# A product-key expert layer on one core: 40 tokens in row dots, two chunks searched together, and the x rows stored in five pieces

## What is computed

```python
q = (xf @ w_query).reshape(t, PEER_HEADS, 2, HALF_QUERY)            # 512 tokens, 8 heads, two halves
scores = jnp.einsum('thpk,hpnk->thpn', q, sub_keys)                 # 128 keys for each half
v1, i1 = lax.top_k(scores[:, :, 0], PEER_TOPK)                      # 16 best of each half
v2, i2 = lax.top_k(scores[:, :, 1], PEER_TOPK)
cand = (v1[..., :, None] + v2[..., None, :]).reshape(t, PEER_HEADS, PEER_TOPK * PEER_TOPK)
best, pos = lax.top_k(cand, PEER_TOPK)                              # 16 best pairs
experts = (e1 * N_KEYS + e2).reshape(t, PEER_HEADS * PEER_TOPK)     # 128 experts of 16384 for a token
gates = jax.nn.softmax(best, axis=-1).reshape(t, PEER_HEADS * PEER_TOPK)
a = jax.nn.gelu(jnp.einsum('cd,ced->ce', xc, expert_u[ic])) * gc    # a dot with each chosen row of u
out = jnp.einsum('ce,ced->cd', a, expert_v[ic])                     # the sum of the rows of v
```

## Time and profile before

| | us |
|---|---|
| median of 3 runs | 1601.42 (1600.41 to 1601.59) |
| the profiled execution | 1600.42 |
| its span in the trace | 1598.6 |
| U phase, first to last matmul of the 128 tiles | 520.5 to 1066.9 |

### The profile page before, as it was taken

The page is one execution under the profiler, slowest core; times in us unless marked ns, Lnnn a source line. Parts: engine busy times, 40 slices in busy tenths (PEclk is TensorE's granted clock), DMA queues, the critical chain, the costliest instruction groups (busy, mean ns, idle before and its releaser), DMA issues.

```text
span 1598.6 us, 25446 instructions
## 1 busy us (share of the span) xinstructions
PE 1588.1 (99%) x8590; PEld 1403.5 (88%) x8590; DVE 1291.2 (81%) x2373; ACT 701.3 (44%) x936; POOL 410.8 (26%) x345
## 2 busy tenths in 40 slices
PE   9999999999999999999999999999999999999998
PEld 8888888888888999999999999998888888888886
DVE  6967833334578888988999998779999999999997
ACT  5444533333334433334677676433334333333334
POOL 1011100000000111103332322544454555455451
PEclk9999999999999999999999999999999999999999
DMA  5477632223322799967999999999999999999994
GB/s 215 146 245 241 232 105 101 96 92 106 109 85 71 243 321 349 333 211 272 330 410 397 392 389 383 409 357 368 387 405 400 409 413 403 398 411 397 400 368 158
DMA packets 150269, 461.82 MB, mean 289 GB/s; under 512 B 15888, under 2 KB 46656, under 8 KB 148544
## 3 DMA queue, kind: packets, MB, share of 16 engines
q1 hardware_dynamic: 82080, 231.08, 39.4%
q0 software_dynamic: 47920, 174.12, 28.8%
q10 hardware_dynamic: 20208, 55.94, 9.2%
HBM read 402.78 MB, written 58.29 MB: 288 GB/s over the span
## 4 chain that ended last, share of the span: by engine, by line
PE 97%; DMA 1%; ACT 1%; DVE 1%; issue 0%; SPq 0%; DVEq 0%; ACTq 0%
PE bank L1032 20%; PE bank L1033 20%; PE bank L1034 20%; PE bank L1220 11%; PE bank L1219 11%; PE bank L1218 11%; PE bank L1195 3%; PE bank L1098 1%; DMA w_lo<-early_dram 1%; DMA h_t<-x_t 1%; PE bank L1232 0%; ACT w_hi L685 0%; DVE w_lo L1271 0%; PE bank L1077 0%; PE bank L1079 0%
## 5 line engine op out<-in xcount | busy, mean ns | idle before, releaser
L685 ACT ACTIVATE w_hi<-w_raw 128x1024 fp32r<-128x1024 f32 x347 | 365.9, 1056 | 349.1 <-PE bank L1220 237.0
L1271 DVE TENSOR_TENSOR w_lo<-w_raw,w_hi 128x1024 fp32r<-128x1024 f32 x329 | 401.6, 1221 | 138.7 <-ACT w_hi L685 131.8
L1032 PE MATMUL bank<-xn_hi,w_hi 128*128 128x352 f32 (+1 forms) x1472 | 510.5, 347 | 2.7 <-DMA w_lo<-early_dram 2.7
L1033 PE MATMUL bank<-xn_lo,w_hi 128*128 128x352 f32 (+1 forms) x1472 | 504.7, 343 | 0.0
L1034 PE MATMUL bank<-xn_hi,w_lo 128*128 128x352 f32 (+1 forms) x1472 | 504.7, 343 | 0.0
L597 POOL DMA_INDIRECT rows<-u_rows,expert x128 | 156.1, 1220 | 646.8 <-DVE expert L1699 353.9
L1218 PE MATMUL bank<-w_hi,a_hi 128*128 128x512 f32 x768 | 298.8, 389 | 0.0
L1220 PE MATMUL bank<-w_hi,a_lo 128*128 128x512 f32 x768 | 298.8, 389 | 0.0
L1219 PE MATMUL bank<-w_lo,a_hi 128*128 128x512 f32 x768 | 298.8, 389 | 0.0
L1032 PEld LDWEIGHTS bank<-xn_hi,w_hi 128*128 128x128 f32 x1472 | 276.7, 188 | 20.7 <-issue 3.5
L1034 PEld LDWEIGHTS bank<-xn_hi,w_lo 128*128 128x128 f32 x1472 | 276.6, 188 | 17.6
(11 more groups left out here) (239 smaller groups left out, 1466.5 us busy)
## 6 DMA issues: line engine op xcount, KB each, us to landing
w_raw<-u SPq DMA_DIRECT2D x128, 512.0 KB
w_raw<-v SPq DMA_DIRECT2D x128, 512.0 KB
g_dram<-g_sb ACTq DMA_DIRECT2D x12, 2048.0 KB
g_in<-g_dram SPq DMA_DIRECT2D x84, 256.0 KB
act_dram<-act_out ACTq DMA_DIRECT2D x54, 352.0 KB
act_in<-act_dram SPq DMA_DIRECT2D x54, 352.0 KB
w_raw<-gate SPq DMA_DIRECT2D x32, 512.0 KB
w_raw<-w_in SPq DMA_DIRECT2D x31, 512.0 KB
```

The lines of the kernel that those rows point to most:

```text
L685: act.activation(w_hi[:, slot, :], w_raw[:, slot, :], ACT.Copy).then_inc(hi_done, 1)
L1032: pe.matmul(out, hi, x_hi, start=k == 0, stop=False)
L1033: pe.matmul(out, hi, x_lo, start=False, stop=False)
L1271: dve.tensor_tensor(w_lo[:, slot, :], w_raw[:, slot, :], w_hi[:, slot, :].bitcast(F32), ALU.subtract).then_inc(lo_done, 1)
```

## The change

1. EXTRA goes from 32 to 40: the dense tokens are 344, the gathers 168, the x rows five groups of 8 tokens.
2. Three-part gates for 48 tokens (MASKS_X 2 to 3): one more of the masks is made in three bf16 products, where other masks have two.
3. `search` takes two chunks and goes through its phases alternately for both; `hold_at` waits for an older mark of VectorE's own count. Chunks 0 and 1 go together, then 2 and 3, each through four pairs of heads. The last dot ahead of the rounds and the rest of the splits stand elsewhere (BEFORE_FIRST 52 to 44, DOTS_BEFORE from 7 entries with 8 dots to 16 entries with 24; dots among the searches from 16 to 9). The exp is at tile 46, the turning ahead of tile 52.
4. The x rows are stored by five DMAs of 8 tokens each (512 KB) at q = 4 to 8, and loaded at q = 10 and 11.
5. Around it: the dots left for the V phase are 46 where they were 48, x_last has memory of its own, extra_rows lies in expert_last's memory.

```diff
-EXTRA = 32
+EXTRA = 40
-EXP_AT = 54
+TURN_AT = 13
-MASKS_X = EXTRA // MASKED
+MASKS_X = -(-EXTRA // MASKED)
+THREE_PARTS = MASKED * MASKS_X
...
+DOTS_FIRST = 1
+DOTS_SEARCH = (1, 1, 1, 2)
+DOTS_DECODE = (1, 1, 1, 1)
+BEFORE_FIRST = 44
+EXP_AT = BEFORE_FIRST + 2
-DOTS_BEFORE = (1, 1, 1, 2, 1, 1, 1)
+DOTS_BEFORE = (2, 1, 2, 1, 2, 2, 1, 2, 2, 1, 1, 1, 1, 2, 2, 1)
...
-X_STORED, X_LOADED = 6, (12, 16)
+X_STORED = (4, 5, 6, 7, 8)
+X_LOADED = (10, 11)
...
+    def mark(self):
+        return self.base + self.count
+
+    def hold_at(self, mark, carrier):
+        self.engine.wait_ge(self.sem, mark)
+        self.engine.sem_inc(carrier, 1)
...
+            def store_x(g):
+                at = P - EXTRA + g * SHARED
+                pool.dma_start(x_rows_dram[g * SHARED:(g + 1) * SHARED, :, :],
+                               x_last[at:at + SHARED, :].unsqueeze(1).broadcast_to([SHARED, SPREAD, D])
+                               ).then_inc(x_rows_stored, 16)
...
-                if q == X_STORED:
-                    pool.dma_start(x_rows_dram, x_last[P - EXTRA:, :].unsqueeze(1).broadcast_to([EXTRA, SPREAD, D])
-                                   ).then_inc(x_rows_stored, 16)
+                if q in X_STORED:
+                    store_x(X_STORED.index(q))
                 if q in X_LOADED:
-                    pool.wait_ge(x_rows_stored, 16)
+                    pool.wait_ge(x_rows_stored, 16 * EXTRA_GROUPS)
...
-            def search(c, i, at, splits):
+            def search(chunks, i, splits):
...
-                for k, u, half in rows_of:
-                    chain.did(dve.max(top_v[:, half, u, 0:8], row(k)))
-                chain.hold(held)
+                for s in both:
+                    for k, u, half in rows_of:
+                        chain.did(dve.max(top_v[:, s, half, u, 0:8], row(s, k)))
+                    done[s] = chain.mark()
+                for s in both:
+                    chain.hold_at(done[s], held)
+                    for k, u, half in rows_of:
+                        chain.did(dve.max_index(index(s, half, u)[:, 0:8], top_v[:, s, half, u, 0:8], row(s, k)))
+                        chain.did(dve.match_replace(less[:, s, k, :], top_v[:, s, half, u, 0:8], row(s, k), LOWEST))
+                    done[s] = chain.mark()
+                    splits[s]()
...
+            decode(1, 4, 1, turns(*QUERY_DECODES[3]))
+            dve.wait_ge(x_tok_ready, 2)
+            rows_done = next_dots(rows_done, DOTS_FIRST)
+            for i in range(PAIRS_OF_HEADS):
+                search((2, 3), i, turns(*LAST_SPLITS[i]))
+                rows_done = next_dots(rows_done, DOTS_SEARCH[i])
+                if i % 2 == 1:
+                    for s in range(2):
+                        decode(2 + s, 2 * (i - 1), s, turns(*LAST_DECODES[i - 1 + s]))
+                        rows_done = next_dots(rows_done, DOTS_DECODE[i - 1 + s])
...
+                if n == EXP_AT + 1:
+                    normalise()
+                if n == SLOTS * TURN_AT + 1:
+                    split_gates()
+                    mask_half(0, False)
+                if n == SLOTS * TURN_AT + 2:
+                    mask_half(0, True)
+                split_tiles(1)
+                u_dots(rows_done + sum(DOTS_BEFORE[:n - BEFORE_FIRST]), count)
```

More of the change, by code:

```diff
@@ L1171, in _ @@
                 last.then_inc(turned, 1)
-            for b in range(SLOTS // 2, SLOTS):
-                u_tile(ONEHOT_AT - 1, b)
+            with pe.Fori(TURN_AT, ONEHOT_AT) as step:
+                for b in range(SLOTS):
+                    u_tile(step, b)
             pe.sem_inc(onehots_used, SLOTS)
@@ L1538, in u_split @@
                     split_weight(SLOTS * step + (AT_U + SLOTS + b), b)
-            def search(c, i, at, splits):
-                keep, v = at
+            def search(chunks, i, splits):
+                v, done = i % 2, [0, 0]
+                both = (0, 1)
                 rows_of = [(k, k // 2, k % 2) for k in range(4)]
[L1544 to L1547, removed]
-                for k, u, half in rows_of:
-                    chain.did(dve.max(top_v[:, half, u, 0:8], row(k)))
-                chain.hold(held)
[L1552 to L1584, removed]
@@ new lines, in search @@
+                row = lambda s, k: scores[:, chunks[s], 4 * i + k, :]
+                top = lambda s, u: best[:, chunks[s], 2 * i + u, :]
+                index = lambda s, half, u: top_i[:, s, half, v, u, :]
+                place = lambda s, u: pos[:, s, v, u, :]
+                for s in both:
[9 more added lines that the diff above has]
+                    splits[s]()
@@ new lines, in search @@
+                for s in both:
+                    chain.hold_at(done[s], held)
+                    for k, u, half in rows_of:
+                        chain.did(dve.max(top_v[:, s, half, u, 8:16], less[:, s, k, :]))
+                    done[s] = chain.mark()
+                for s in both:
+                    chain.hold_at(done[s], held)
+                    for k, u, half in rows_of:
+                        chain.did(dve.max_index(index(s, half, u)[:, 8:16], top_v[:, s, half, u, 8:16], less[:, s, k, :]))
+                    for first, count, width, start in ((0, TOP_A, TOPK, 0), (TOP_A, TOPK - TOP_A, LOW_B, WIDE)):
+                        part = [P, 2, count, width]
+                        chain.did(dve.tensor_tensor(
+                            cand[:, s, :, start:start + count * width].rearrange("p u (a b) -> p u a b", a=count),
+                            top_v[:, s, 0, :, first:first + count].unsqueeze(3).broadcast_to(part),
+                            top_v[:, s, 1, :, 0:width].unsqueeze(2).broadcast_to(part), ALU.add))
+                    done[s] = chain.mark()
+                    splits[2 + s]()
@@ new lines, in search @@
+                for s in both:
+                    chain.hold_at(done[s], held)
+                    for u in range(2):
+                        chain.did(dve.max(top(s, u)[:, 0:8], cand[:, s, u, :]))
+                    done[s] = chain.mark()
+                for s in both:
+                    chain.hold_at(done[s], held)
+                    for u in range(2):
+                        chain.did(dve.max_index(place(s, u)[:, 0:8], top(s, u)[:, 0:8], cand[:, s, u, :]))
+                        chain.did(dve.match_replace(cand_less[:, s, u, :], top(s, u)[:, 0:8], cand[:, s, u, :], LOWEST))
+                    done[s] = chain.mark()
@@ new lines, in search @@
+                splits[4]()
+                for s in both:
+                    chain.hold_at(done[s], held)
+                    for u in range(2):
+                        chain.did(dve.max(top(s, u)[:, 8:16], cand_less[:, s, u, :]))
+                    done[s] = chain.mark()
+                splits[5]()
+                for s in both:
+                    chain.hold_at(done[s], held)
+                    for u in range(2):
+                        chain.did(dve.max_index(place(s, u)[:, 8:16], top(s, u)[:, 8:16], cand_less[:, s, u, :]))
@@ L1722, in _ @@
             dve.tensor_tensor(best[:], best[:], over_ranks(denom), ALU.subtract).then_inc(shifted, 1)
-            before_done = [0]
-            def before_masks(count):
-                for _ in range(count):
-                    n = before_done[0]
-                    split_tiles(1)
-                    u_dots(rows_done + sum(DOTS_BEFORE[:n]), DOTS_BEFORE[n])
-                    before_done[0] += 1
-            before_masks(2)
-            dve.wait_ge(exp_ready, CHUNKS)
-            chain.did(dve.tensor_reduce(denom[:], best[:], AX.X, ALU.add))
```

166 lines of the change are left out of this document (79 added, 87 removed).

## The result

The changed kernel takes 1618.7 us (1617.36 to 1619.81, 4 runs) against 1600.97 for the one before, a ratio of 1.011 with a 95% interval of 1.0093 to 1.0128. It is slower by 17.7 us; the forecast was 1592.7, and the measured time lies beyond the range too. The profiled execution took 1619.71 us with a span of 1617.9.

A forecast was written before the change was run, and what follows sets the result against it. TensorE, busy 99% of the span, was taken as the bound: 1600.42 - 10.1 + 0.9 - 3.0 + 2.5 + 1.0 = 1591.7 us profiled, 1592.7 for the median. The 8-in-10 range was 1588 to 1611.

The forecast's parts named there:

- The bound by TensorE: Whole kernel: TensorE is busy 99% of the span, so only its own work and its waits set the time.
- the old stall: Early tiles behind the single x-row store: TensorE stood still twice, 3.0 us together, which goes with that store: -3.0.
- The store in five pieces: GpSimd's x-row stores: each piece holds the queues some 5 us and loses 0.5 us, +2.5 in all, bounds 0 and 27.
- the upper bound: X-row pieces from 8 partitions: 51 GB/s, each holding the queues 10.2 us, as long as the whole store.
- Rival one: Tiles 13 to 33: each piece holds the queues 10.2 us, early loads come late, 1605.2 to 1617 us; chance 0.33.
- Rows late: Tiles 44 to 59 and the last tiles: rows reach VectorE late as DMA turns full, 0.5 us each, +1.0.
- Rival three: Tiles 44 to 59 and last tiles: pieces cheap, rows 3 us later, TensorE loses 5 us, 1597 us; chance 0.08.
- 2% of 60 us: Tiles 44 to 59: 421 GB/s asked where 414 was reached, so rows 1 us late at the end; 0.5 taken.
- The last tiles: End of the kernel: TensorE gains on rows paced by DMA, leaving 0.5 us of slack; 0.5 taken, bounds 0 and 1.5.
- Fewer columns: U tiles: 3072 matmuls, each 8 columns narrower at 0.41 ns a column, all on the path: -10.1 us.
- Three parts: Masks in the rounds: one more three-part mask gives two tiles 24 one-hot matmuls instead of 16: +0.9 us.
- Search of two chunks: VectorE's searches: alternating chunks covers most waits, gaining 20 of 26 us of VectorE's time; price on the path 0.

The follow-up runs named there:

- experiment 1: The changed kernel, with each x row stored once and the five pieces copied from DRAM to DRAM instead of read from SBUF: 1598.89 us.
- experiment 5: The changed kernel, with each of the five pieces taking every fifth token (8 partitions apart) instead of 8 neighbours: 1599.92 us.
- experiment 3: The kernel before, with only its store of x rows cut into four pieces of 8 tokens at q = 4 to 7: 1608.07 us.
- Experiment 6: Four dots moved from tiles 44 to 59 into the searches, on experiment 1 (1595.27 us) and on experiment 5 (1594.70 us); then two dots fewer (1592.48 us).
- experiment 8: The kernel before, with U tiles of slots 0 to 3 at 352, 344, 336 and 328 columns: tiles last 3.84, 3.78, 3.70 and 3.60 us.
- the last run of experiment 6: The changed kernel with strided pieces, four dots moved into the searches and two dots fewer in tiles 48 to 51: 1592.48 us.

## Why the prediction was wrong

**The bound by TensorE, and the old stall.** Right. The waits for early tiles decided the case, as the earlier trace rows had told.

**The store in five pieces.** This is the step that failed. I gave a piece 5 us and 0.5 us of loss. It takes 10 us, the upper bound, and the five cost 15.0 us of waits and 4.7 of low clock, against 3.2 before. Experiments 1 and 5 took the cause away in two ways, and the stall went both times. The number to go by stood in the earlier trace rows: 205 GB/s from 32 partitions. The estimate of 51 GB/s for 8 neighbours, worked out from it with the page "SBUF — State Buffer" of the Trainium skill (section "Door 1: The DMA port swizzle"), is what was measured. I set against it that pieces are spaced by dots and that a hold shorter than the lead of 11.3 us need not stop TensorE. The old store spoke against that already: a hold of 10 us had made a load take 14.10 us, longer than the hold and than the lead. Of two bounds, with a row and an estimate both pointing at one end, the middle was no forecast.

**Rival one** named the mechanism, and gave 1605 to 1617. It was the right one in what a piece costs, though a piece does not shut the other queues out as the old store did. The time still lies above its range: it lacked the clock and the lateness below.

**The low clock.** Not in the prediction at all. The row of before had 1.00 throughout, with waits of at most 1.4 us. Waits of 4 to 6 us brought the clock down, 6.2 us in all with tile 63. The wait of 2.9 us at tile 17 did not, but the length of a wait does not settle it: in experiments 1 and 3 the clock fell behind waits of 1.9 and 2.4 us.

**Rows late.** Rival three, with 5 us, was nearly right and is not a rival but an addition: 5.9 us at tiles 62 and 63 and 2.6 us more, where the sum had 1.0. In experiment 1, without the stall, 4.5 us of waits for VectorE and their clock remain. VectorE waits 10.4 us for rows from 700 to 790 us in the changed kernel and had no such wait there before. Experiment 6 settles that 24 dots with the split of the gates behind tile 52 were too many for that stretch. The step that was mis-sized is "2% of 60 us": the rows come late in ten waits of up to 2.3 us, not by the mean rate. The last tiles cost 1.8 us for the 0.5 I took (bounds 0 and 1.5).

**Fewer columns.** The mechanism was right and the size off: -6.8 us for -10.1. The slope between 352 and 512 columns is not that between 344 and 352, since 344 lies above the line (experiment 8).

**Three parts.** Right: six tiles with 24 one-hot matmuls, 5.23 us instead of 4.77, +0.9.

**Search of two chunks.** Right that nothing of it is on the path. Most of the waits are covered: five waits for its own results are left in the searches, the longest of 1.3 us. The gain was put too high. By the starts and ends of VectorE's instructions the searches of before lost 14 us to such waits, mostly 0.15 us each and not 0.24, and those of the changed kernel 4 us: some 10 us gained, where I took 20 of 26. What it is worth in time could not be seen by itself; no run has the old search with the new rest. The diff has 10 dots among the searches, not 9 as written ahead of the prediction; nothing hangs on it.

With the strided pieces and fewer dots (the last run of experiment 6) the change gives 1592.48 us, 8 us below the kernel before. In the U phase of its profile the columns give 6.8 us and the old stall 3.2; the mask takes 0.9, and late w_lo in the last tiles 1.7. That this meets the forecast of 1592.7 is luck: the columns gave 3.3 us less than the sum had, and the pieces cost nothing where it had 2.5.

## What to carry to other kernels

Before a DMA is cut into pieces, look at which SBUF partitions each piece reads: pieces of neighbouring partitions can be as long as the whole, and loads that share the engines come late by them. Cut across the partitions (by stride or by repeats) instead, and keep a piece short against the lead of the loads that matter. Add the clock to the price of a stall of TensorE: it was low at all eight waits of 3.9 us and more in these runs, and behind some of about 2 us. When a table fills a stretch to the full rate of a resource, expect single waits of some us rather than the mean shortfall.

## What the runs showed of the hardware that was not expected

- A store by GpSimd's queue from 8 neighbouring partitions: 0.59 us for a packet of 4 KB; every fifth partition: at most 0.22 us, the rows of a gather among them; 32 neighbours: 0.31 us.
- Behind idle stretches of 4.1, 4.5 and 5.7 us matmuls of 344 columns started 0.28 to 0.29 us apart instead of 0.16 for part of a tile; behind 2.9 us they did not, and behind 1.9 us (experiment 1) and 2.4 us (experiment 3) the clock fell as well.
- fp32 matmuls of 352, 344, 336 and 328 columns start 160.0, 157.7, 154.1 and 150.0 ns apart: the first columns left out save the least, all 24 together 0.41 ns each.
- A copy from DRAM to DRAM of 2 MB in one DMA still made TensorE wait 1.6 us for one load; five of 0.5 MB, in the changed kernel, did not.
